# Expert weights of a decoder trunk loaded as 8 KB runs per partition, with strided transposes of the activations

## The chip, the core and the metric

The kernel runs on one core of a Trainium2 chip. Its time is the device time of one execution in microseconds (us). Before the change three runs took 1944.39, 1949.98 and 1954.2 us; the median is 1949.98 us.

The engines are named PE or TensorE (matrix products; PEld is its weight load), DVE or VectorE, ACT or ScalarE, POOL or GpSimd, and SP, which only issues transfers. Partition means one of the 128 rows of the on-chip memory.

## The reference

One inference step of a two-layer decoder trunk, for 512 prompt tokens and 32 sample tokens together (544 rows of 1024 channels). Each layer has a mixer, a cross attention over 256 memory tokens and a mixture of experts; after each comes a residual sum and a layer norm. The change touches the mixture of experts alone:

```python
def hier_moe(x, w_group, b_group, w_router, b_router, w_gate, w_up, w_down):
    ...                       # gates: a token's best group, its two best experts in it
    hg = jnp.einsum('md,edf->mef', xf, w_gate)     # 16 experts, d = 1024, f = 512
    hu = jnp.einsum('md,edf->mef', xf, w_up)
    hid = jax.nn.silu(hg) * hu * gates.astype(x.dtype)[..., None]
    y = jnp.einsum('mef,efd->md', hid, w_down)
```

All arrays are 32-bit floats. A product sums over all contraction rows, so the order in which these rows are dealt out to partitions is free, as long as both operands use the same order.

## The kernel before

Every matrix product is made from operands split in a high and a low part: for each weight tile ScalarE copies `raw` (128 x 2048) to `whi` in the product's rounded format (line 1308 in the expert loops), VectorE makes the rest, `wlo = raw - whi` (line 1685), and TensorE adds three products, hi x hi, lo x hi and hi x lo (line 924).

Weights come in units of 1 MB through a ring of four `raw` buffers. SP issues the loads in program order; a load into a buffer waits until VectorE has made the low part of the unit that was there before (`wait_release`). An expert has six units: two halves of `w_gate`, two of `w_up`, two of `w_down` (`expert_load`, line 461, issue at line 469). For `w_gate` a unit holds 512 contraction rows of 512 values, four rows on each partition; for `w_down` it holds 256 rows of 1024 values, two on each partition. In the kernel before, row `(u k p)` of an expert lies on partition p, so the rows of one partition are 128 rows apart in the memory outside: a gate or up unit is 512 runs of 2 KB, a down unit 256 runs of 4 KB.

Each expert handles up to 128 tokens. The order of one step of the loop over experts, on each engine: VectorE compares ranks to find the slots of a later expert (`hits`, line 1769) and turns TensorE's sums (line 901) into a list of token numbers (`tokens`, line 1778). GpSimd waits for this list, does a one-element operation (line 2176), and issues an indirect transfer that gathers 128 rows of 4 KB from the outside copy of the activations into `xg` (line 2177). TensorE transposes the gathered rows, 8 blocks of 128 x 128 (line 910); ScalarE and VectorE copy the blocks out as a high and a low part. TensorE then runs the gate and up products (48 matrix products of 512 columns), waits for the gathered rows of the next expert and transposes them, runs the down product of the expert before (24 products, line 924 too), transposes the hidden rows of this one (4 blocks, line 953), and sums the slots of the expert after next. VectorE forms the hidden rows (line 1799) after the split of the next expert's gate units. ScalarE writes the expert's result to `ye` (line 1356) and issues its store to `expert_rows` (line 1364). Steps are in program order on every engine, joined by counting semaphores; the loops are unrolled for the first three and last three experts and run in pairs between.

Tokens that don't fit in the 128 slots of an expert are handled after the loop, in `further` (lines 972 to 1035), with the same layout and unsplit products. In these data layer 1 has one such block.

A transpose is a product in which the data are the stationary operand and the identity matrix moves past it; the profile's names stand as moving, stationary.

Of the kernel before, what the change touches and what calls it, by code (L numbers as in the profile page):

```python
# [31 lines left out]
P = 128  # L32

def trunk_kernel(nc, a, outs):
    D = a["x_prompt"].shape[2]
# [5 lines left out]
    EXPERTS, FF = a["w_gate"].shape[1], a["w_gate"].shape[3]  # L42
# [6 lines left out]
    KC = D // P  # L49
# [150 lines left out]
    with ExitStack() as ctx:  # L200
# [25 lines left out]
        ident = sb("ident", [P, P])  # L226
# [37 lines left out]
        ps = ctx.enter_context(nc.psum_tensor("ps", [P, 8, 512], F32))  # L264
# [51 lines left out]
        xg = [area(1024 * i, 1024) for i in range(2)]  # L316
        silu = area(2048, 512)
        hid = area(2560, 512)
# [33 lines left out]
        A_, B_, C_, D_ = range(4)  # L352

        def pair_flat(i):
            return PAIR[i].rearrange("p b n -> p (b n)")

        def pair_chunks(i):
            return pair_flat(i).rearrange("p (k n) -> p k n", k=KC)
# [78 lines left out]
        @block.sync  # L437
        def _(sp):
            sp.dma_start(mem_rows, a["mem_prompt"][0].rearrange("(m p) n -> p m n", p=P)).then_inc(sig("mem_landed"), 16)
            i_raw = 0  # L440
            for u in UNITS:
                if u[0] == "unit":
                    _, key, src, wait_kv = u
                    if wait_kv:

                        for par in range(2):
                            sp.wait_ge(sig(f"kv_stored{par}"), 16 * 2 * DEPTH)
                    wait_release(sp, i_raw)
                    for dst, part in src(raw[i_raw % RING][:, :]):
                        sp.dma_start(dst, part).then_inc(sig(f"raw_landed{i_raw % RING}"), 16)  # L450
                    i_raw += 1
                    if key == ("wk0", 3):
                        sp.dma_start(h[:, 0:LASTT, :], a["x_prompt"][0].rearrange("(t p) n -> p t n", p=P)).then_inc(sig("x_landed"), 16)
                        sp.dma_start(h[0:NS, LASTT, :], a["x_sample"].rearrange("b t n -> (b t) n")).then_inc(sig("x_landed"), 16)
                    continue
                l, rb = u[1], i_raw
                w_gate = a["w_gate"][l].rearrange("e (u k p) n -> u e p k n", u=2, p=P)
                w_up = a["w_up"][l].rearrange("e (u k p) n -> u e p k n", u=2, p=P)
                w_down = a["w_down"][l].rearrange("e (u k p) n -> u e p k n", u=2, p=P)

                def expert_load(k, i, w, e):

                    wait_release(sp, rb + k, 12 * i)
                    slot = (rb + k) % RING
                    if isinstance(e, int):
                        src = w[e]
                    else:
                        src = w[bass.ds(e, 1)].rearrange("a p k n -> (a p) k n")
                    sp.dma_start(raw[slot][:, :].rearrange("p (k n) -> p k n", k=src.shape[1]), src).then_inc(sig(f"raw_landed{slot}"), 16)

                def load_step(c, i):
                    k, n = first_unit(c), c + 2 * i
                    if c < EXPERTS:
                        expert_load(k, i, w_gate[0], n)
                        expert_load(k + 1, i, w_gate[1], n)
                        expert_load(k + 2, i, w_up[0], n)
                        expert_load(k + 3, i, w_up[1], n)
                        k += 4
                    if c:
                        expert_load(k, i, w_down[0], n - 1)  # L480
                        expert_load(k + 1, i, w_down[1], n - 1)

                load_step(0, 0)
                for c in range(1, 3):
                    load_step(c, 0)
                with sp.Fori(0, EXPERTS // 2 - 3) as i:
                    load_step(3, i)
                    load_step(4, i)
                for c in range(EXPERTS - 3, EXPERTS + 1):
                    load_step(c, 0)  # L490
                i_raw += 6 * EXPERTS
                n = further_blocks(sp, l)
                def one_block(i):
                    e = sp.value_load(block_expert[0:1, i:i + 1] if isinstance(i, int) else block_expert[0:1, bass.ds(i, 1)], min_val=0, max_val=EXPERTS - 1)
                    for k, w in enumerate((w_gate, w_up, w_down)):
                        for q in range(2):
                            if k == 2:

                                sp.wait_ge(again(l, "used"), 2 + q + 6 * i)
                            elif isinstance(i, int):  # L500
                                wait_release(sp, i_raw + 2 * k + q)
                            elif k == q == 0:

                                sp.wait_ge(again(l, "used"), 1 + 6 * i)
                            src = w[q][bass.ds(e, 1)].rearrange("a p k n -> (a p) k n")
                            sp.dma_start(again_slot(l, 2 * k + q)[:, :].rearrange("p (k n) -> p k n", k=src.shape[1]), src).then_inc(again(l, f"landed{q}"), 16)

                with sp.If(n > 0):
                    one_block(0)
                with sp.If(n > 1):  # L510
                    with sp.Fori(1, FURTHER) as i:
                        with sp.If(n > i):
                            one_block(i)
                if l < DEPTH - 1:

                    sp.wait_ge(again(l, "used"), 1 + 6 * n)
# [3 lines left out]
        def _(pe):  # L520
# [110 lines left out]
            n = 0  # L631
# [259 lines left out]
            def experts(l):  # L891
# [12 lines left out]
                def gathered_columns(c, i):  # L904
                    n = c + 2 * i
                    pe.wait_ge(sig(f"gathered{c % 2}"), 16 * (l * EXPERTS // 2 + c // 2 + 1) + 16 * i)
                    if c:
                        pe.wait_ge(sig(f"xg{l}_lo"), past(f"xg{l}_lo") + n)
                    for k in range(KC):
                        mm = pe.transpose(pair_chunks(C_)[:, k, :], xg[c % 2][:, k * P:(k + 1) * P], ident[:, :])  # L910
                    mm.then_inc(sig(f"xg{l}_tr"), 1)

                def expert_product(k0, i, bank, hi, lo, k_unit, nbanks):
# [14 lines left out]
                def step(c, i):  # L928
                    n, k = c + 2 * i, first_unit(c)
                    if c < EXPERTS:  # L930

                        pe.wait_ge(sig(f"xg{l}_hi"), past(f"xg{l}_hi") + n + 1)
                        pe.wait_ge(sig(f"xg{l}_lo"), past(f"xg{l}_lo") + n + 1)
                        if c:
                            pe.wait_ge(sig(f"hid{l}"), past(f"hid{l}") + n)
                        expert_product(k, i, 0, xgT_hi, xgT_lo, 4, 1)
                        expert_product(k + 2, i, 1, xgT_hi, xgT_lo, 4, 1)
                        k += 4
                    if c < EXPERTS - 1:
                        gathered_columns(c + 1, i)  # L940
                    if c:

                        pe.wait_ge(sig(f"hid{l}_hi"), past(f"hid{l}_hi") + n)
                        pe.wait_ge(sig(f"hid{l}_lo"), past(f"hid{l}_lo") + n)
                        if c > 1:
                            pe.wait_ge(sig(f"ye{l}"), past(f"ye{l}") + n - 1)
                        expert_product(k, i, 2, hidT_hi, hidT_lo, 2, 2)
                    if c < EXPERTS:
                        pe.wait_ge(sig(f"hid{l}"), past(f"hid{l}") + n + 1)
                        if c:  # L950
                            pe.wait_ge(sig(f"hid{l}_lo"), past(f"hid{l}_lo") + n)
                        for k in range(4):
                            mm = pe.transpose(ps[:, 6, k * P:(k + 1) * P], hid[:, k * P:(k + 1) * P], ident[:, :])
                        mm.then_inc(sig(f"hid{l}_tr"), 1)
                    if c < EXPERTS - 2:
                        find_tokens(c + 2, i)
# [15 lines left out]
            def further(l):  # L972
# [3 lines left out]
                n = further_blocks(pe, l)  # L976
                def one_block(i):
# [9 lines left out]
                    pe.wait_ge(again(l, "copied"), 1 + 4 * i)  # L987
                    pe.wait_ge(again(l, "gathered"), 16 + 16 * i)
                    for k in range(KC):
                        mm = pe.transpose(pair_chunks(C_)[:, k, :], xg[0][:, k * P:(k + 1) * P], ident[:, :])  # L990
                    mm.then_inc(again(l, "tr"), 1)

                    pe.wait_ge(again(l, "copied"), 2 + 4 * i)
# [8 lines left out]
                            mm.then_inc(again(l, "used"), 1)  # L1002
                    pe.wait_ge(again(l, "hid"), 1 + i)
                    for k in range(4):
                        mm = pe.transpose(ps[:, 6, k * P:(k + 1) * P], hid[:, k * P:(k + 1) * P], ident[:, :])
                    mm.then_inc(again(l, "tr"), 1)

                    pe.wait_ge(again(l, "copied"), 3 + 4 * i)
# [1338 lines left out]
```

## Time and profile before

| | us |
|---|---|
| median of three runs | 1949.98 |
| lowest and highest | 1944.39, 1954.2 |
| span of the profiled execution (first to last instruction; the only time given of it) | 1949.7 |

| engine | busy us | share of the span | instructions |
|---|---|---|---|
| PE | 1591.0 | 82% | 8295 |
| PEld | 1278.4 | 66% | 8295 |
| DVE | 1178.7 | 60% | 1285 |
| ACT | 720.8 | 37% | 646 |
| POOL | 411.8 | 21% | 405 |

The two loops over experts lie at about 560 to 900 us and 1505 to 1850 us. The profile comes as a page and as a trace that can be asked for stretches, waits and the chain of work that ended last. The DMA share is the mean busy share of the core's 16 transfer engines; queue q1 carries what SP issues, q10 what ScalarE issues, q0 what GpSimd issues.

### The profile page before, as it was taken

Reading aid. Unit: us, or ns where it says so; the run is one execution under the profiler, and the core shown is the slowest. Engines: PE = TensorE matmul, PEld = TensorE weight load, DVE = VectorE, ACT = ScalarE, POOL = GpSimd, SP = SyncE. Lnnn points to the kernel's source line nnn. Section 1 sums busy time; section 2 is a strip of 40 time slices with the busy share of each in tenths; the row PEclk is TensorE's granted clock in tenths of the full one; section 3 lists DMA queues with packets and bytes.
Section 4 is the critical chain, followed back from the end, with each engine's and each line's share of the span. In section 5 each row is a group of like instructions: output and inputs, shape, how many; then the busy total and the mean of one; then the engine's idle time right before and its main releaser. Section 6 shows DMA issues by size and latency. Waiting matters only on the chain.

```text
span 1949.7 us, 21407 instructions
## 1 busy us (share of the span) xinstructions
PE 1591.0 (82%) x8295; PEld 1278.4 (66%) x8295; DVE 1178.7 (60%) x1285; ACT 720.8 (37%) x646; POOL 411.8 (21%) x405
## 2 busy tenths in 40 slices
PE   7989798899959999994496559898995899989860
PEld 5888478865647777773396557787673677777730
DVE  4333552341658788785779994513336787877636
ACT  4331321330236676673111112223202567666500
POOL 0101121000211001012689922300012000100006
PEclk9999798999979999997597779999998899999985
DMA  9730302066148999997411120203634699999822
GB/s 319 271 130 22 113 18 73 23 251 224 33 169 319 361 366 346 360 364 237 118 58 51 43 68 32 88 23 110 252 113 154 223 365 356 346 363 360 313 97 94
DMA packets 157539, 371.69 MB, mean 191 GB/s; under 512 B 8597, under 2 KB 38325, under 8 KB 157441
## 3 DMA queue, kind: packets, MB, share of 16 engines
q1 hardware_dynamic: 137200, 307.38, 44.9%
q0 software_dynamic: 12672, 44.76, 6.3%
q10 hardware_dynamic: 7585, 18.42, 2.6%
q8 instruction: 57, 0.93, 0.2%
q14 instruction: 25, 0.20, 0.0%
HBM read 342.54 MB, written 28.59 MB: 190 GB/s over the span
## 4 chain that ended last, share of the span: by engine, by line
PE 48%; DVE 21%; DMA 12%; issue 8%; POOL 4%; ACT 4%; ACTq 1%; DVEq 0%; SPq 0%; POOLq 0%
PE ps L543 15%; PE ps L924 10%; DMA arena<-h_rows,tok_of 6%; PE ps L560 6%; DMA raw<-in_w_gate_dram 4%; DVE arena L1969 3%; PE ps L832 3%; PE ps L847 3%; DVE arena L1967 3%; DVE wlo L1685 3%; DVE wlo L1481 2%; DVE xlo L1484 2%; ACT whi L1308 2%; PE ps L760 2%; PE ps L576 2%
## 5 line engine op out<-in xcount | busy, mean ns | idle before, releaser
L1685 DVE TENSOR_TENSOR wlo<-raw,whi 128x2048 fp32r<-128x2048 f32 x192 | 436.7, 2288 | 125.7 <-ACT whi L1308 124.9
L1308 ACT ACTIVATE whi<-raw 128x2048 fp32r<-128x2048 f32 x192 | 366.7, 1916 | 178.8 <-DMA raw<-in_w_gate_dram 86.9
L924 PE MATMUL ps<-whi,xhi 128*128 128x512 f32 x768 | 296.1, 413 | 18.2 <-issue 9.0
L924 PE MATMUL ps<-whi,xlo 128*128 128x512 f32 x768 | 287.4, 402 | 0.0
L924 PE MATMUL ps<-wlo,xhi 128*128 128x512 f32 x768 | 286.6, 400 | 0.0
L1481 DVE TENSOR_TENSOR wlo<-raw,whi 128x2048 fp32r<-128x2048 f32 x56 | 130.0, 2335 | 94.0 <-ACT whi L1151 94.0
L924 PEld LDWEIGHTS ps<-whi,xhi 128*128 128x128 f32 x768 | 147.1, 195 | 51.7 <-issue 18.0
L543 PE MATMUL ps<-whi,xhi 128*128 128x512 f32 (+1 forms) x528 | 170.1, 404 | 8.2 <-DVE wlo L1481 6.3
L924 PEld LDWEIGHTS ps<-whi,xlo 128*128 128x128 f32 x768 | 149.5, 195 | 34.1
L924 PEld LDWEIGHTS ps<-wlo,xhi 128*128 128x128 f32 x768 | 147.8, 192 | 35.6
L1484 DVE TENSOR_TENSOR xlo<-ps,xhi 128x1024 fp32r<-128x1024 f32 (+2 forms) x112 | 110.0, 983 | 97.3 <-ACT xhi L1155 34.4
L543 PE MATMUL ps<-wlo,xhi 128*128 128x512 f32 (+1 forms) x528 | 165.8, 395 | 0.0
L543 PE MATMUL ps<-whi,xlo 128*128 128x512 f32 (+1 forms) x528 | 165.4, 394 | 0.0
L560 PE MATMUL ps<-xhi,whi 128*128 128x272 f32 x544 | 119.0, 302 | 47.9 <-DVE rt L1987 46.6
L2176 POOL TENSOR_TENSOR wait_mark<-minus_half 1x1 f32<-1x1 f32 x32 | 29.1, 911 | 555.0 <-DVE tok_of L1778 541.6
L1151 ACT ACTIVATE whi<-raw 128x2048 fp32r<-128x2048 f32 x56 | 106.3, 1911 | 87.4 <-PE ps L560 61.3
L560 PEld LDWEIGHTS ps<-xhi,whi 128*128 128x128 f32 x544 | 90.5, 200 | 49.3 <-DVE rt L1987 47.9
L560 PE MATMUL ps<-xlo,whi 128*128 128x272 f32 x544 | 117.5, 299 | 0.0
L1155 ACT ACTIVATE xhi<-ps 128x1024 fp32r<-128x1024 f32 (+1 forms) x32 | 28.9, 905 | 238.5 <-PE ps L528 238.5
L560 PE MATMUL ps<-xhi,wlo 128*128 128x272 f32 x544 | 116.9, 297 | 0.0
L543 PEld LDWEIGHTS ps<-whi,xhi 128*128 128x128 f32 (+1 forms) x528 | 93.0, 180 | 36.2 <-issue 9.0
L543 PEld LDWEIGHTS ps<-whi,xlo 128*128 128x128 f32 (+1 forms) x528 | 94.0, 178 | 30.0
(319 smaller groups left out, 2347.2 us busy)
## 6 DMA issues: line engine op xcount, KB each, us to landing
raw<-in_w_gate_dram SPq DMA_DIRECT2D x66, 1024.0 KB, 7.4
raw<-in_w_up_dram SPq DMA_DIRECT2D x66, 1024.0 KB, 7.8
raw<-in_w_down_dram SPq DMA_DIRECT2D x66, 1024.0 KB, 7.4
raw<-in_cache_mem_k_dram SPq DMA_DIRECT2D x16, 1024.0 KB, 5.3
raw<-in_cache_mem_v_dram SPq DMA_DIRECT2D x16, 1024.0 KB, 5.6
expert_rows<-arena ACTq DMA_DIRECT2D x32, 512.0 KB
raw<-in_w_k_dram SPq DMA_DIRECT2D x8, 1024.0 KB, 8.6
raw<-in_w_v_dram SPq DMA_DIRECT2D x8, 1024.0 KB, 10.3
```

What stands on the lines that cost most here:

```text
L543: mm = pe.matmul(ps[0:m, 2 * pair + half, :], x[:, k, lhs_cols], w[s % RING][:, at:at + 512], start=(k == 0 and n == 0), stop=(k == KC - 1 ...
L560: mm = pe.matmul(ps[:, 2 * pair + half, 0:MOVE], w[s % RING][:, at:at + P], x[:, k, half * MOVE:(half + 1) * MOVE], start=(k == 0 and n == ...
L832: mm = pe.matmul(pair[0:NS, hh * NMEM:(hh + 1) * NMEM], q_only[:, j, b, :], KT[(b + 1) % 2][:, j, :], start=(b == 0 and j in (0, 4)), stop ...
L847: mm = pe.matmul(pair_flat(A_)[0:NS, hh * HD:(hh + 1) * HD], p_only[:, 2 * hh + m, b, :], vb[:, m, hh * HD:(hh + 1) * HD], start=(b == 0 a ...
L924: mm = pe.matmul(ps[:, bank + half, :], x[:, k, :], w[s][:, at:at + 512], start=(k == 0 and n == 0), stop=(k == 2 * k_unit - 1 and n == 2))
L1151: act.activation(whi[s % RING][:, :], raw[i % RING][:, :], ACT.Copy).then_inc(sig("hi_made"), 1)
L1308: act.activation(whi[s % RING][:, :], raw[r % RING][:, :], ACT.Copy).then_inc(sig("hi_made"), 1)
L1481: dve.tensor_tensor(wlo[s % RING][:, :], raw[i % RING][:, :], whi[s % RING][:, :].bitcast(F32), ALU.subtract).then_inc(sig("lo_made"), 1)
L1484: return dve.tensor_tensor(out, full, hi.bitcast(F32), ALU.subtract)
L1685: dve.tensor_tensor(wlo[s % RING][:, :], raw[r % RING][:, :], whi[s % RING][:, :].bitcast(F32), ALU.subtract).then_inc(sig("lo_made"), 1)
L1967: written["p"] = link.mark(dve.scalar_tensor_tensor(p_out, p_in, w, p_out, ALU.mult, ALU.add))
L1969: ins = dve.scalar_tensor_tensor(s_out, s_in, w, s_out, ALU.mult, ALU.add)
```

## The change

The rows of an expert are dealt to the partitions in another order: partition p takes 8 rows of `w_gate` and `w_up` (4 of `w_down`) that follow each other, and a unit takes half of them. Each partition's share of a unit is then one run of 8 KB. To match, block k of the transposed activations holds channels k, k + 8, k + 16 and so on (for the hidden rows k, k + 4, ...) in place of 128 that follow each other.

```diff
-                w_gate = a["w_gate"][l].rearrange("e (u k p) n -> u e p k n", u=2, p=P)
-                w_up = a["w_up"][l].rearrange("e (u k p) n -> u e p k n", u=2, p=P)
-                w_down = a["w_down"][l].rearrange("e (u k p) n -> u e p k n", u=2, p=P)
+                w_gate = a["w_gate"][l].rearrange("e (p u k) n -> u e p k n", u=2, p=P)
+                w_up = a["w_up"][l].rearrange("e (p u k) n -> u e p k n", u=2, p=P)
+                w_down = a["w_down"][l].rearrange("e (p u k) n -> u e p k n", u=2, p=P)
...
-                        mm = pe.transpose(pair_chunks(C_)[:, k, :], xg[c % 2][:, k * P:(k + 1) * P], ident[:, :])
+                        mm = pe.transpose(pair_chunks(C_)[:, k, :], xg[c % 2][:, k:D:KC], ident[:, :])
...
-                            mm = pe.transpose(ps[:, 6, k * P:(k + 1) * P], hid[:, k * P:(k + 1) * P], ident[:, :])
+                            mm = pe.transpose(ps[:, 6, k * P:(k + 1) * P], hid[:, k:FF:4], ident[:, :])
```

The two transposes of the extra blocks (lines 990 and 1005) change in the same way.

## Rows read from the trace of the kernel before

**Rows 1.** The page's chain that ended last, share of the span by line.
```profile
PE ps L543 15%; PE ps L924 10%; DMA arena<-h_rows,tok_of 6%; PE ps L560 6%; DMA raw<-in_w_gate_dram 4%; DVE arena L1969 3%; PE ps L832 3%; PE ps L847 3%; DVE arena L1967 3%; DVE wlo L1685 3%; DVE wlo L1481 2%; DVE xlo L1484 2%; ACT whi L1308 2%; PE ps L760 2%; PE ps L576 2%
```
**Rows 2.** Busy us (instructions) per engine, clock, DMA share, GB/s: the expert loops.
```profile
620.00:900.00 280.00, 259.60 (x1210) 208.83 (x1208) 221.80 (x146) 190.37 (x135) 28.23 (x25) 0.98 1.00 356
...
1560.00:1810.00 250.00, 230.90 (x1077) 186.17 (x1076) 201.61 (x134) 172.43 (x122) 27.05 (x24) 0.97 0.98 355
```
**Rows 3.** Chain in order of time, two experts of layer 0: start us, us, what.
```profile
778.05 8.96 DMA raw<-in_w_gate_dram
...
791.27 0.68 DVE arena L1799
...
796.19 2.32 POOL wait_mark L2176
...
798.65 9.10 DMA arena<-h_rows,tok_of
...
807.79 1.09 PE ps L910 x8
808.88 5.58 PE ps L924 x24
...
816.22 1.92 ACT whi L1308
...
820.48 6.95 DMA raw<-in_w_gate_dram
```
**Rows 4.** The chain in both expert loops: first and last transfers on it.
```profile
594.86 6.39 DMA arena<-h_rows,tok_of
...
615.49 7.34 DMA raw<-in_w_gate_dram
...
1504.56 4.26 DMA arena<-h_rows,tok_of
...
1540.13 6.44 DMA arena<-h_rows,tok_of
...
1725.67 7.25 DMA raw<-in_w_gate_dram
...
1784.80 8.88 DMA arena<-h_rows,tok_of
```
**Rows 5.** Waits in 620:900 of PE and ACT: us in total, times, longest.
```profile
PE ps L910 <- DMA arena<-h_rows,tok_of: 12.2, 6, 2.9
...
ACT whi L1308 <- DMA raw<-in_w_gate_dram: 37.8, 21, 3.4
```
**Rows 6.** DMA in 1181:1192, where a cache copy of 8 blocks runs.
```profile
DMA packets 320, 1.47 MB, mean 134 GB/s; under 512 B 56, under 2 KB 56, under 8 KB 312
```
**Rows 7.** DMA in 235:238 (1 KB), 643:646 (2 KB) and 10:16 (4 KB).
```profile
DMA packets 1096, 1.11 MB, mean 369 GB/s; under 512 B 15, under 2 KB 1096, under 8 KB 1096
...
DMA packets 598, 1.20 MB, mean 399 GB/s; under 512 B 18, under 2 KB 18, under 8 KB 598
...
DMA packets 660, 2.50 MB, mean 416 GB/s; under 512 B 50, under 2 KB 50, under 8 KB 660
```
**Rows 8.** DMA queues (packets, MB, share) in 804:805, then in 50.5:51.5.
```profile
q0 software_dynamic: 66, 0.27, 69.0%
q1 hardware_dynamic: 63, 0.13, 34.2%
...
q0 software_dynamic: 54, 0.22, 53.7%
q1 hardware_dynamic: 51, 0.21, 50.7%
```
**Rows 9.** Instructions of lines 910, 1713 (16-byte steps), 1756: ns min/median/max, starts, forms.
```profile
L910 PEld LDWEIGHTS ps<-ident,arena x256: 137/141/231, 563.8 to 1815.5; 128*128 128x128 f32 x128
...
L1713 DVE TENSOR_REDUCE picked<-arena x2: 289/290/290, 551.8 to 1497.3; 128x20 f32<-128x80 f32 x2
...
L1756 DVE TENSOR_REDUCE rt<-arena x4: 235/236/236, 561.3 to 1508.1; 128x5 f32<-128x80 f32 x4
```

More of the change, by code:

```diff
@@ L989, in one_block @@
                     for k in range(KC):
-                        mm = pe.transpose(pair_chunks(C_)[:, k, :], xg[0][:, k * P:(k + 1) * P], ident[:, :])
+                        mm = pe.transpose(pair_chunks(C_)[:, k, :], xg[0][:, k:D:KC], ident[:, :])
                     mm.then_inc(again(l, "tr"), 1)
@@ L1004, in one_block @@
                     for k in range(4):
-                        mm = pe.transpose(ps[:, 6, k * P:(k + 1) * P], hid[:, k * P:(k + 1) * P], ident[:, :])
+                        mm = pe.transpose(ps[:, 6, k * P:(k + 1) * P], hid[:, k:FF:4], ident[:, :])
                     mm.then_inc(again(l, "tr"), 1)
```

## The prediction

> **What bounds the kernel now.** I read the chain of waits first, then the stretches, then the waits of single engines, and last the DMA queues. The page's chain says that no engine holds the end alone; among its largest pieces stand the gather of token rows (6% of the span) and the load of expert gate weights (4%), both transfers of the expert loops [rows 1]. The change lives in those two loops. There the DMA engines are busy all the time (share 1.00 and 0.98, 356 and 355 GB/s) and TensorE is busy 259.60 of 280 us and 230.90 of 250 us, so both have little left [rows 2]. An expert lasts 20.4 us: the gather of the third expert of layer 1 starts at 1540.13, that of the fifteenth at 1784.80 [rows 4].
>
> A piece of the chain, two experts long, shows the loop that sets the pace [rows 3]. Weights land (8.96 us), are split by ScalarE and VectorE, VectorE makes the hidden rows, then the token list; GpSimd marks (2.32) and issues the gather; the gather lands after 9.10 us; TensorE transposes the gathered rows (1.09), does the down product (5.58); the split of the next weights frees a slot, and the next gate load goes out. So the path passes through two transfers per pair of experts, a weight load and a gather. The same alternation runs through both loops: 12 gathers that meet weights stand on the chain from 594.86 to 1784.80, together 101.8 us, 8.5 each, and 10 weight loads from 615.49 to 1725.67, together 77.2 us, 7.7 each [rows 4]. The gather at 1504.56, which meets no weight stream, needs 4.26 us, half of the others. In the loop of layer 0 TensorE waits for the gather in every second expert, 12.2 us in six waits, and ScalarE for gate weights, 37.8 us in 21 [rows 5].
>
> **The change, part by part.**
>
> *Fewer, longer packets.* A gate or up load is 512 runs of 2 KB now and 128 of 8 KB after; a down load 256 of 4 KB and then 128 of 8 KB. A run of that length can be one packet: in the stretch with the cache copy (8 blocks of 53 KB) all but 312 of 320 packets are under 8 KB, so the eight blocks are one packet each [rows 6]. What a packet costs beyond its bytes I take from three full streams: 369 GB/s with 1 KB packets, 399 with 2 KB, 416 with 4 KB [rows 7]. Over 16 engines that is 44.4, 82.1 and 157.5 ns a packet, which is a straight line: 37.7 ns per KB and 6.7 ns fixed. An 8 KB packet is then an estimated 308 ns (426 GB/s). A 1 MB load takes 32 packets an engine x 82.1 = 2.63 us now and 8 x 308 = 2.46 after, 0.16 less; a down load 2.52 to 2.46. Per expert 4 x 0.16 + 2 x 0.06 = 0.76 us, 24 us over 32 experts: that is the whole gain if the transfers alone set the pace. On the chain only the 10 weight legs count. Each waits for about two loads' worth of moving (2 x 0.16 = 0.3), and loses less to gathers that cut in (next paragraph; up to 0.65 us). I take 0.6 a leg: -6 us (bounds 0 and -10).
>
> *The gather against longer packets.* Two queues that both have work share an engine packet by packet, not byte by byte. Where 4 KB rows meet 4 KB rows, 54 and 51 packets pass in one us and each side gets half the time; where gathered 4 KB rows meet 2 KB weights, 66 and 63 packets pass, and the gather gets 69.0% against 34.2% [rows 8]. So the gather is favoured today because its packets are the longer ones. After the change they are the shorter ones. An engine carries 8 rows of a gather. Now that is 8 x (0.167 + 0.087) = 2.0 us (times per packet from the same rows: 69.0% of 16 us over 66, 34.2% over 63); after, 8 x (0.167 + 0.308) = 3.8 us. So a gather that meets weights lands 1.8 us later. In the experts where it is already late, nothing hides this: TensorE stands at the transposes behind it, in order, and the down product, the hidden rows' transposes and the token search of the next experts are queued behind those. 12 legs x 1.8 = +21.6 us. Bounds: 0 if a long run gives way inside itself as often as now, and 12 x 3 = +36 if rows in flight ahead of the first one add as much again. The write of expert rows is slowed in the same way, but nothing waits for it in the loop.
>
> A part comes back: with each pair of experts longer by some 1.6 us of 41, the streams have 4% less to carry per us, and the two legs (7.7 and 8.5 us) shorten by about that: 0.65 a pair, -8 us over 12 pairs. This is an estimate; the bounds are 0 and -16.
>
> *Strided transposes.* The gathered rows and the hidden rows are the stationary operand, so the stride falls on the weight load of TensorE: 141 ns for 128 columns today, all contiguous [rows 9]. No row shows a strided load on TensorE. The nearest is VectorE reading the same memory: a reduction over 80 values 16 bytes apart takes 290 ns, over 80 adjacent ones 236 [rows 9], 0.67 ns a value more, though it also writes 20 results and not 5. For 128 columns that is 86 ns a load. Bounds: 0, and a doubling of the load (141 ns). I take 86, because it is the only row that differs by the stride. There are 12 such loads per expert, but only the 8 behind a gather that is on the chain count in full: 14 legs (the 12 and the first of each loop) x 8 x 0.086 = +9.6 us, and 12 in the extra block of layer 1, +1.0. The other loads lie in experts where TensorE has the 2 to 3 us of its next wait for a gather as cover; without it they would cost another 14 us. The Trainium skill, page "SBUF — State Buffer", section Specifications (TRN2), says that memory lines are 16 bytes and that full bandwidth needs at least two hits in a line; both new strides (32 and 16 bytes) put each value in a line of its own, so by the page the loads slow down, by an amount that it doesn't give, and without that rule the sum is 10 us lower. No run here shows it for TensorE.
>
> *Unchanged.* Buffers, semaphores, the order of issue on SP and POOL and the number of DMA instructions stay. The splits of weights read the same contiguous 128x2048 tiles.
>
> Sum: -6 + 21.6 - 8 + 9.6 + 1.0 = +18 us on the profiled span of 1949.7, which lies 0.3 us under the median of the runs shown (1949.98): 1968 us.
>
> **The rivals.**
> 1. *Faster: the stream sets the pace.* The share of 1.00 speaks for it, and ScalarE's waits for gate weights. Then the 0.76 us per expert come through, and the gather loses little because the weights are further ahead: -24 us without stride cost, 1926. The limit is TensorE, busy 92.5% of the loop. Against it: single weights are waited for by ScalarE, hardly by TensorE [rows 5]. It decides if a gather under load still lands in 9 us or less. Chance 0.28.
> 2. *No change.* The packets save on the weight leg what the gather loses: gather +0.7 us (as beside 4 KB packets: 8 x (0.167 + 0.157) = 2.6 against 2.0), so 12 x 0.6 = +7, -6 for the weight legs, no stride cost: 1951. The same number comes out if the runs stay cut at 2 KB, so that the change doesn't do what it says, and the loads of TensorE don't care for the stride. Chance 0.18.
> 3. *Slower by TensorE.* The strided load takes twice its time, 141 ns x 12 = 1.7 us an expert. TensorE has 1.5 us idle per expert (280 - 259.60 us over 280 / 20.4 experts), so it becomes the bound in both experts of a pair, with the gather's delay on top: 1968 + 32 x 1.7 - 10 = about 2012. For it: every value in another line. Against it: the load overlaps the multiplication before it. Chance 0.12.
>
> The forecast itself has 0.42.
>
> **How the numbers follow.** What a measurement of this kernel can tell from no change is about 0.5%, 10 us. The forecast's own range, from the bounds of its four terms (half widths 5, 18, 8 and 6, squared, summed and rooted: 21), is 1947 to 1989, so about 0.04 of its 0.42 lies within 0.5% of before. Slower by more than that: 0.38 and rival 3, 0.50; within: 0.18 and 0.04, 0.22; faster: 0.28. For 8 in 10 the range must reach into rival 1 and most of the way to rival 3: 1926 to 2006.
>
> **What would show it.** Packets of 8 KB in the expert loops, some 28,700 fewer per layer (16 experts x (4 x 384 + 2 x 128)). One us in which gather and weights meet should show equal packet counts but the gather at about a third of the time; gathers under load at 10 to 11 us; weight loads at 7 us or a little less; the wait of TensorE for the gather at twice its 12.2 us. The loads of lines 910 and 953 at 200 to 230 ns and not 140. The forecast is wrong if gathers land as before or the waits of TensorE shrink, and its stride part if those loads still take 140 ns.

## The result and the profile after

The changed kernel takes 1956.64 us (median of 20 runs, 1947.9 to 1963.6), the kernel before 1950.76 (20 runs). The ratio is 1.0039, 95% interval 1.0021 to 1.0057: slower by 4 to 11 us. The forecast was slower by 18 us, 1968. The profiled execution has a span of 1957.9 us against 1949.7.

The chain of the page names the place. The columns are those of [rows 1]:

```profile
PE ps L543 16%; PE ps L924 8%; DMA arena<-h_rows,tok_of 8%; PE ps L560 6%; DMA raw<-in_w_gate_dram 4%; DVE arena L1969 3%; DVE wlo L1685 3%; PE ps L832 3%; PE ps L847 3%; DVE arena L1967 3%; ACT whi L1308 3%; DVE wlo L1481 2%; DVE xlo L1484 2%; PE ps L760 2%; PE ps L910 2%
```

The gather went from 6% to 8% of the chain, and line 910, the transposes that wait for it, came into the list. The windows of the two loops, columns as in [rows 2]:

```profile
620.00:900.00 280.00, 258.81 (x1186) 210.62 (x1185) 219.84 (x145) 190.01 (x133) 26.28 (x25) 0.96 0.94 352
...
1566.00:1816.00 250.00, 227.66 (x1051) 185.85 (x1050) 195.58 (x130) 169.20 (x118) 25.54 (x24) 0.95 0.93 347
```

Fewer instructions of TensorE fit in the same window (1186 for 1210 in layer 0), the transfer engines have become idle 6% of the time, and the bytes per us have fallen a little, 356 to 352. So the packets did get cheaper (the price of a megabyte stands below), and yet no more bytes pass. How long each loop lasts shows from the transposes of the hidden rows, one group of four per expert. Line 953, columns: ns min/median/max, first and last start, forms; before, layer 0 and layer 1:

```profile
L953 PE MATMUL ps<-ident,arena x64: 270/273/330, 582.9 to 892.3; 128*128 128x128 f32 x64
...
L953 PE MATMUL ps<-ident,arena x64: 270/272/330, 1528.2 to 1839.8; 128*128 128x128 f32 x64
```

and after:

```profile
L953 PE MATMUL ps<-ident,arena x64: 272/284/386, 580.3 to 893.4; 128*128 128x128 f32 x64
...
L953 PE MATMUL ps<-ident,arena x64: 272/284/387, 1529.4 to 1847.7; 128*128 128x128 f32 x64
```

First to last start is 309.4 and 311.6 us before, 313.1 and 318.3 after: 10.4 us more in the two loops; the rest of the program lies 2.2 us the other way.

The packets are what the diff says (page, section on queues; before there were 157539 packets):

```profile
DMA packets 98403, 371.69 MB, mean 190 GB/s; under 512 B 8597, under 2 KB 38325, under 8 KB 72961
```

The chain of waits in both loops, start us, us, what; first the gather that meets no weights, then the first and last of those that do, and the first and last weight leg (they answer to [rows 4]):

```profile
1505.77 4.27 DMA arena<-h_rows,tok_of
...
592.31 6.68 DMA arena<-h_rows,tok_of
...
1792.26 9.80 DMA arena<-h_rows,tok_of
...
613.31 6.53 DMA raw<-in_w_gate_dram
...
1773.49 7.43 DMA raw<-in_w_gate_dram
```

There are 14 gathers that meet weights on the chain, 139.9 us together, 10.0 each (before 12, 8.5 each), and 12 weight legs, 81.9 us, 6.8 each (before 10, 7.7 each). So not only the length of a leg changed, but their number: gather and weight load now alternate without a gap through both loops, where the chain of before skips a gather in places (gate loads at 675.86 and 694.80 follow each other). The free gather is as it was, 4.27. TensorE's and ScalarE's waits in 620:900, us in total, times, longest, beside [rows 5]:

```profile
PE ps L910 <- DMA arena<-h_rows,tok_of: 17.2, 6, 3.8
...
ACT whi L1308 <- PE ps L924: 32.0, 31, 3.7
ACT whi L1308 <- DMA raw<-in_w_gate_dram: 30.1, 19, 2.9
```

The wait for the gather is up by 5.0 us, ScalarE's wait for gate weights down by 7.7: waiting moved from the one transfer to the other. The strided loads show in line 910's records, 193 ns for the 141 of [rows 9]:

```profile
L910 PEld LDWEIGHTS ps<-ident,arena x256: 185/193/231, 560.9 to 1823.8; 128*128 128x128 f32 x128
```

### The profile page after: what moved, and what is told of

It is laid out like the page before. It is cut to its first block, busy times and chain, and to the rows that moved or that the text cites. A ratio compares the mean times of both kernels' runs of the same rounds, so it can differ in the third digit from the quotient of the medians.

```text
span 1957.9 us, 21407 instructions
## 1 busy us (share of the span) xinstructions
PE 1596.4 (82%) x8295; PEld 1286.2 (66%) x8295; DVE 1178.4 (60%) x1285; ACT 722.1 (37%) x646; POOL 408.3 (21%) x405
## 4 chain that ended last, share of the span: by engine, by line
PE 47%; DVE 22%; DMA 14%; issue 7%; ACT 5%; POOL 4%; ACTq 0%; DVEq 0%; POOLq 0%; SPq 0%
PE ps L543 16%; PE ps L924 8%; DMA arena<-h_rows,tok_of 8%; PE ps L560 6%; DMA raw<-in_w_gate_dram 4%; DVE arena L1969 3%; DVE wlo L1685 3%; PE ps L832 3%; PE ps L847 3%; DVE arena L1967 3%; ACT whi L1308 3%; DVE wlo L1481 2%; DVE xlo L1484 2%; PE ps L760 2%; PE ps L910 2%
## 5 line engine op out<-in xcount | busy, mean ns | idle before, releaser
L2176 POOL TENSOR_TENSOR wait_mark<-minus_half 1x1 f32<-1x1 f32 x32 | 17.9, 558 | 567.5 <-DVE tok_of L1778 554.1
## 6 DMA issues: line engine op xcount, KB each, us to landing
raw<-in_w_v_dram SPq DMA_DIRECT2D x8, 1024.0 KB, 10.6
```

## The experiments

The theory: a gather that meets 8 KB runs lands 1.5 us later, on the chain 0.9 us per weight leg comes back, and the strided loads of TensorE cost nothing because they hide. Rival A: the stride makes the time. Rivals B to G stand with the runs for which they were written. All ratios are against the kernel before on the same chip; they and their intervals come from all runs of both kernels and need not be the ratio of the two medians.

**The changed kernel again**, as the base of this set.

> The changed kernel as it is, as the base for the others on the same chip. All theories: 1.003 to 1.005 of the kernel before (about +6 us). Gathers that meet weights at 10.0 us on the chain (8.5 before), weight legs at 6.8 us (7.7 before).

1961.36 us, ratio 1.0041 (1.0010 to 1.0072). Twelve gathers that meet weights are on the chain, 9.8 us each, and seven weight legs of 7.2 us. The amount of the loss holds; the legs of single executions differ by some tenths.

**Stride alone.**

```diff
-                w_gate = a["w_gate"][l].rearrange("e (p u k) n -> u e p k n", u=2, p=P)
+                w_gate = a["w_gate"][l].rearrange("e (p k u) n -> u e p k n", u=2, p=P)
...
-    xg[c % 2][:, k:D:KC]
+    xg[c % 2][:, 2 * (k % 4) + k // 4:D:KC]
```

(`w_up`, `w_down` and the other three transposes in the same way.)

> Stride without length: the rows of a partition are dealt so that the transposes are strided as in the change, but the runs stay 2 KB (gate, up) and 4 KB (down), as before. Theory (the gather loses the favoured half of the transfer engines to longer runs, and the strided loads hide behind the transpose before them): as the kernel before, 1951 +- 3 us, gathers under load back at 8.5 us, equal packet counts of gather and weights where they meet, the wait of TensorE for the gather in layer 0's loop near 12 us; loads of lines 910 and 953 at 185 to 210 ns all the same. Rival A (the stride on TensorE makes the time): as the changed kernel, 1957 us, with gathers at 8.5 us. Rival B (the +6 us are a shift of which experts fall late, not tied to either part): anything between 1945 and 1960 with gathers at 8.5 to 9.

1948.89 us, 0.9995 (0.9968 to 1.0021). Every transpose is strided, its load is recorded as long as in the changed kernel, and nothing is lost:

```profile
L910 PEld LDWEIGHTS ps<-ident,arena x256: 185/193/231, 565.5 to 1811.4; 128*128 128x128 f32 x128
```

Ten gathers under load are on the chain, 7.8 us each, 0.7 us under the kernel before at an equal time; so a mean of some ten legs can move by that much without the length of the gate runs. Rival A falls, and so does the forecast's +10.6 us for the stride: the interval allows -6 to +4.

**Half the length.**

```diff
-                w_gate = a["w_gate"][l].rearrange("e (p u k) n -> u e p k n", u=2, p=P)
+                w_gate = a["w_gate"][l].rearrange("e (p g u j) n -> u e p g (j n)", u=2, g=2, p=P)
```

(`w_up` alike, `w_down` as in the run above, the transposes to match.)

> Half the length: strided as in the change, all weight runs 4 KB. Theory in its present form (a long run gives way about every 4 KB): the gather shares as beside 8 KB runs, so gathers at 9.5 to 10 us, one packet of weights for one of the gather, time 1955 to 1958 us. Rival C (a run of 8 KB passes whole, as the prediction had it): gathers here near 9 us (8 x (0.167 + 0.157) = 2.6 us an engine against 2.0 before), clearly below the 10.0 of 8 KB runs, and 1952 to 1954 us. Rival A: 1957 us with gathers at 9.

1970.07 us, 1.0095 (1.0057 to 1.0133): slower than with 8 KB, which none of the theories had. Gathers on the chain take 8.9 us, as rival C said, so their length doesn't explain it. More of this below.

**Length without stride, in layer 1.**

```diff
-    xg[c % 2][:, k:D:KC]
+    xg[c % 2][:, k * P:(k + 1) * P] if l else xg[c % 2][:, k:D:KC]
```

> Length without stride, in layer 1 alone: runs of 8 KB everywhere, but layer 1's transposes read contiguous columns (so layer 1's expert products pair other channels with the weight rows than the reference does; the amount of work and the routing are the same). Theory: as the changed kernel within 2 us (eight transposes behind a gather 1.09 and not 1.16 us, 0.07 x 7 legs), gathers of layer 1 still near 10.5 us. Rival A: layer 1's loop, 7 us longer in the change from its third to its last expert (272.8 against 265.8 us), gets these 7 us back, so the time is back at 1950 to 1951 us.

(The hidden rows and the extra block in the same way.) 1960.69 us, 1.0061 (1.0035 to 1.0088): by the medians 0.7 us under the changed kernel of the same set, by the ratios 0.2% above it, so nothing is regained. The recorded loads of line 910 go from 137 ns (layer 1) to 193 (layer 0) in one kernel, and TensorE waits for layer 1's gathers as long as in the changed kernel (18.8 us there):

```profile
PE ps L910 <- DMA arena<-h_rows,tok_of: 19.8, 7, 3.8
```

What the stride costs where it is on the chain can be read directly. Eight transposes and the products behind them, changed kernel, layer 0 (strided, start us, us, what):

```profile
765.06 1.16 PE ps L910 x8
766.22 5.57 PE ps L924 x24
```

and this kernel, layer 1 (contiguous):

```profile
1635.88 1.09 PE ps L910 x8
```

The recorded load grows by 52 ns, eight transposes in a row by 0.07 us, 9 ns each. That holds at TensorE's full clock. Behind many waits for a gather it runs at half of it (last section), and where it does so throughout, eight take 1.97 us strided or not; in the kernel before (contiguous) for example:

```profile
642.95 1.97 PE ps L910 x8
```

**Only `w_down` in 8 KB runs** (gate and up as before).

> Only w_down in 8 KB runs (hidden rows transposed with stride), gate and up as before in 2 KB runs; a third of the weight bytes change. Theory (long runs stretch the time in which a gather's rows pass): gathers on the chain at 8.5 to 9 us, those that meet a down load longest; time between before and the changed kernel, 1950 to 1954 us. Rival D (the loss has another cause than the gather, and goes with the bytes in long runs): a third of +8 us, 1952 us, with gathers at 8.5 us. Both give nearly one time, the legs tell them apart.

1956.02 us, 1.0031 (1.0007 to 1.0056). Gathers on the chain 8.7 us (13 legs), weight legs 7.8: the gate loads that are on the chain give nothing back here, and the gather loses 0.2 us a leg. That makes less than the 8 us between the medians, but the interval reaches down to 1.4 us, and the execution with these legs, 1969.01 us, was the slowest of the twelve. The run doesn't tell the theories apart.

**The gather taken off the chain.** On TensorE the token search of expert c + 2 moves from the end of the step to right behind the gate and up products, on VectorE the token list from the start of the next step to right behind the hidden rows. GpSimd then issues the gather earlier: by the packet records of the kernels with 2 KB runs, in layer 0's loop, its first row starts 7.5 to 11.1 us ahead of the transposes that use it and not 2.4 to 5.0 (some 5 us more, and not the 10 that were expected). Two kernels: this edit on the changed kernel and on the kernel before.

```diff
                         k += 4
+                    if c < EXPERTS - 2:
+                        find_tokens(c + 2, i)
                     if c < EXPERTS - 1:
                         gathered_columns(c + 1, i)
...
-                    if c < EXPERTS - 2:
-                        find_tokens(c + 2, i)
...
-                    if c and c < EXPERTS - 1:
-                        tokens(c + 1, i)
...
                     dve.tensor_tensor(hid, silu, ps[:, 1, :], ALU.mult).then_inc(sig(f"hid{l}"), 1)
+                    if c < EXPERTS - 2:
+                        tokens(c + 2, i)
```

> The changed kernel, with the token search and the token list of expert c + 2 moved forward by about half an expert (right behind the gate and up products and behind the hidden rows), so that the gather is issued some 10 us earlier against its use. Theory: the gather leaves the chain, TensorE's wait for it in layer 0's loop falls from 17 us to under 4 us, gathers may take 10 us or more without harm, and the saved packet time comes through: DMA share back to 0.97 or more, time 1920 to 1940 us, and faster than the same edit on the kernel before by 8 to 24 us. Rival D: the long runs cost something besides the gather, so this kernel is not faster than the same edit on the kernel before. Rival E (TensorE or the splits hold the loop anyway): waits for the gather vanish, but the time stays within 5 us of the changed kernel.

> The same move of the token search in the kernel before (2 KB and 4 KB runs, contiguous transposes). Theory: there the transfer engines have a share of 1.00 already, so taking the gather off the chain gives little: 1940 to 1950 us, with the wait for the gather gone and ScalarE's wait for gate weights up from 37.8 us. Rival E: as much gain as with long runs or none in both.

With 8 KB runs 1913.31 us, 0.9819 (0.9780 to 0.9857); with the runs of before 1914.36, 0.9820 (0.9786 to 0.9854). The wait for the gather is gone from TensorE's list in 620:900, with 8 KB runs:

```profile
PE ps L924 <- DVE xlo L1484: 4.7, 5, 1.8
PE ps L924 <- issue: 4.5, 8, 0.7
PE ps L955 <- DVE arena L1797: 1.0, 3, 0.4
```

No gather that meets weights is left on the chain of either. They land even later now, and it does no harm: medians of 12 in 620:900, DMA issues, columns out<-in, engine, operation, count, us to landing; 8 KB first, then 2 KB:

```profile
arena<-h_rows,tok_of POOLq DMA_INDIRECT x12, 10.0
```

```profile
arena<-h_rows,tok_of POOLq DMA_INDIRECT x12, 8.5
```

Three things follow. The loss of the changed kernel goes when its gather is covered. The cheaper packets don't turn into time even then: the gate legs on the chain take 8.1 us (14 legs) with 8 KB and 8.0 (15 legs) with 2 KB, and the two kernels have one time, where the theory had 8 to 24 us between them. That is the sign that was written for rival D; whether the saved packet time is worth nothing there or another cost of the long runs eats it up, these runs don't tell. Rival E's reason, that TensorE or the splits hold the loop anyway, falls: both kernels run some 35 us under the kernel before. And my expectation for the kernel before was wrong by 25.6 us or more: I took the share of 1.00 for a full stream. With the same 2 KB runs, the same share and the gather covered, more bytes pass (366 and 370 GB/s against the 356 and 355 of [rows 2]):

```profile
620.00:900.00 280.00, 250.26 (x1180) 199.23 (x1178) 225.28 (x150) 197.08 (x138) 20.73 (x29) 0.97 1.01 366
...
1566.00:1816.00 250.00, 233.72 (x1112) 186.27 (x1110) 204.67 (x142) 173.86 (x123) 19.63 (x29) 0.99 1.00 370
```

The covered loops end earlier, at about 875 and 1798, so these windows hold some of what follows. A window inside both loops shows it more clearly, before and then covered, both with 2 KB runs:

```profile
620.00:840.00 220.00, 204.20 (x965) 164.88 (x964) 179.85 (x121) 154.08 (x109) 26.18 (x22) 0.98 0.99 358
```

```profile
620.00:840.00 220.00, 209.43 (x1000) 167.09 (x999) 189.06 (x127) 163.52 (x116) 13.62 (x24) 0.99 1.02 379
```

**Addresses against length.** 4 KB runs had lost more than 8 KB runs. In all the layouts above with 4 or 8 KB gate runs, a unit is made of alternate pieces of 2 MB. These three make each unit one contiguous megabyte (two of them), or keep the spaced 4 KB runs and cover the gather.

```diff
-    "e (p u k) n -> u e p k n"            # 8 KB runs, 16 KB apart
+    "e (u p k) n -> u e p k n"            # 8 KB runs, contiguous unit
...
-    "e (p g u j) n -> u e p g (j n)"      # 4 KB runs, 8 KB apart
+    "e (u g p j) n -> u e p g (j n)"      # 4 KB runs, contiguous unit; w_down as before
```

> 8 KB runs as in the change, but a unit is one contiguous megabyte (partition p of unit u takes rows 512 u + 4 p to 512 u + 4 p + 3) in place of 128 runs 16 KB apart; transposes read every 4th (hidden: every 2nd) column. Theory (the length of a run is what delays the gather): as the changed kernel, 1.003 to 1.006 of before, gathers on the chain at 10 us. Rival F (the addresses, alternate pieces of 2 MB, slow the loads and not the length): back to the time before, gathers at 8.5 us.

> 4 KB runs for gate and up with each unit one contiguous megabyte; down as before. Earlier, 4 KB runs 8 KB apart gave 1.0095, more than 8 KB runs did, with gathers at only 8.9 us and weight legs at 8.0. Theory (length alone): the same 1.007 to 1.012. Rival F (addresses): 1.000 to 1.004, weight packets passing at 170 us or less per thousand and not 181, weight legs at 7.5 us.

> The 4 KB runs 8 KB apart with the early token search. Theory (whatever the length, the loss passes through the gather on the chain): as the two other kernels with the early search, 1914 +- 4 us, 0.980 to 0.984. Rival F (the 4 KB loads themselves are slow): the loss of 18 us stays, 1925 to 1935 us.

8 KB, contiguous: 1957.94 us, 1.0032 (1.0010 to 1.0055), gathers 10.0 us (14 legs), weight legs 7.1. Here no effect of the addresses shows, and that of the length does. Every kernel with 8 KB gate runs and the gather on the chain loses (1.0032 to 1.0061), stride alone doesn't; against rival B, the loss goes with the length.

4 KB, contiguous: 1944.49 us, 0.9976 (0.9954 to 0.9999), gathers 9.0 us (11 legs), gate legs 7.1 (8 legs); faster than the theory and rival F both had it. With the length kept and the spacing gone (that of `w_down` too), 1.2% of the time comes back, some 23 us. Spaced first, then contiguous, window 620:900 (queue q1: packets, MB, share; issues as above):

```profile
q1 hardware_dynamic: 24478, 84.50, 83.8%
...
raw<-in_w_gate_dram SPq DMA_DIRECT2D x24, 1024.0 KB, 8.4
...
arena<-h_rows,tok_of POOLq DMA_INDIRECT x12, 8.7
```

```profile
q1 hardware_dynamic: 29786, 86.95, 84.2%
...
raw<-in_w_gate_dram SPq DMA_DIRECT2D x24, 1024.0 KB, 7.7
...
arena<-h_rows,tok_of POOLq DMA_INDIRECT x12, 7.6
```

A megabyte takes 83.8% x 280 us x 16 / 84.50 = 44.4 us of engine time spaced and 43.4 contiguous (44.1 and 42.6 in 620:840, which lies inside both loops), and gate loads and gathers land 0.7 and 1.1 us later when spaced. But 44.4 is no more than the 45.1 of the kernel before with 2 KB runs, so the price of a megabyte alone doesn't make the spaced kernel slower than that one.

4 KB, spaced, gather covered: 1946.53 us, 0.9987 (0.9968 to 1.0005), against 1914 for the other layouts. So this layout is slow even without the gather on the chain, as rival F had it and the theory not, and by more than rival F had it (1925 to 1935). ScalarE waits longer for down weights than in the four other kernels with the gather covered (41.4 us against 12.8 to 30.6), and TensorE for the hidden rows (13.5 against 1.0 to 3.0):

```profile
ACT whi L1308 <- DMA raw<-in_w_down_dram: 41.4, 17, 3.6
ACT whi L1308 <- DMA raw<-in_w_gate_dram: 19.9, 23, 2.0
...
PE ps L955 <- DVE arena L1797: 13.5, 13, 1.8
```

Why pieces of 4 KB at a distance of 8 KB are slow and pieces of 8 KB at 16 KB are not stays open. The distance alone isn't it: in the run with stride alone `w_down` already lay in 4 KB pieces 8 KB apart, its loads landed as before (7.5 us), and nothing was lost.

**Contiguous units with the gather covered**, 8 KB and then 4 KB runs.

> 8 KB runs of contiguous units with the early token search. Theory: with the gather off the chain neither length nor stride counts, 1914 +- 4 us. Rival F: some us faster than the early search with 8 KB runs 16 KB apart, 1905 to 1910 us.

> 4 KB runs of contiguous units, the fastest layout without the early token search (0.9976), with it. Theory (with the gather off the chain the length of a run doesn't count, only badly spaced 4 KB runs do): as with 2 KB and 8 KB runs, 0.980 to 0.984, 1910 to 1917 us. Rival G (the gain of contiguous 4 KB runs comes from the loads and not from the gather, so it adds to the early search): 0.977 to 0.980, 1904 to 1910 us. Weight packets of the loads at a mean of 174 us per thousand, as without the early search.

1913.91 us, 0.9818 (0.9789 to 0.9848), and 1915.26 us, 0.9825 (0.9793 to 0.9857). Both medians lie with the theory and outside the ranges of rivals F and G, though both intervals reach into these. Four kernels with the gather covered, with runs of 2, 4 and 8 KB, lie within 2 us, where the same layouts with the gather on the chain spread from 0.9976 to 1.0041. Each interval is some 0.35% wide to either side, so a remainder of a few us can't be excluded for any one of them.

## Why the prediction was wrong in size

The direction and the place hold, and the other terms hold as a net change per leg; the step that failed is "Strided transposes", a term of +10.6 us that measured 1 us or less.

*Fewer, longer packets, and the gather against them: right by the leg, the sum in part by luck.* The forecast had a gather at +1.8 us less half of the 0.65 us per pair that comes back, so about +1.5 a leg, and a weight leg at -0.6 with the other half, about -0.9. Measured: 8.5 to 10.0 and 7.7 to 6.8. These terms alone, -6 + 21.6 - 8, make +7.6 us, or 1957.3; the runs give 1956.64. But they were summed over 12 gathers and 10 weight loads, and the chain of after has 14 and 12: the legs of both kinds grew from 179.0 to 221.8 us together, 42.8 more, while the span grew by 8.2, because other work left the chain in their place. The sum has no term for that; that it comes out to a microsecond is in part luck. The price of the bytes was right too: weights took 86.08 MB in 86.6% of the window before, 45.1 us of engine time a MB, and take 84.87 MB in 80.9%, 42.7, after: 5% less, as the straight line through [rows 7] says for four gate and up units (2.63 to 2.46) and two down units (2.52 to 2.46). The shortest 8 KB packets of the weight loads in the window take 307 ns, where 308 was estimated; their mean is 342.

*Strided transposes: +9.6 and +1.0 forecast, 1 or less measured.* The step took VectorE's 0.67 ns per value for a term of the end time, one load after the other. The loads did grow, by 52 ns in line 910 and 69 in line 953 (86 forecast), but strided loads of 193 ns follow each other every 145 ns (eight in 1.16 us), so the records overlap, and eight in a row took 1.16 us for 1.09. Over 14 legs that is 1 us at most, since at half the clock it is nothing. Two runs show it from both sides: stride without length 0.9995, length without stride in layer 1 no faster than the change. The trace of before could have told: eight transposes take 1.09 us [rows 3], 136 ns each, less than one recorded load of 141 [rows 9], so the records already overlapped, and a longer record need not be a longer pitch. The Trainium skill, "Perfetto Trace Analysis", section "Per-instruction lifecycle: what the profiler-reported window actually captures", says that the end of a TensorE instruction in a profile is worked out from its size and a memory delay, and isn't observed. These traces fit that (193 ns recorded, 145 from one to the next): the pitch is the number to sum, not the record. Two slips of that step leave the forecast where it is: its loads without cover come to 23 us by its own figures (272 of 0.086 us) and not 14, and the half width of its term to 8 and not 6.

*The gather is right by its legs, its mechanism isn't shown.* I expected equal packet counts where rows meet long runs, the gather at a third of the time. One us of the changed kernel (802:803; packets, MB, share) shows two rows to one run and the gather ahead:

```profile
q0 software_dynamic: 48, 0.20, 57.6%
q1 hardware_dynamic: 24, 0.16, 37.8%
```

Slices at 1630 and 1716 look the same (40 to 23, 51 to 25). By the forecast's own sum these counts make 8 x (0.192 + 0.126) = 2.5 us an engine against 2.0, a third of the 1.5 us by which the legs grew; so that one for one gave nearly the right size is luck as far as such slices show. Over the whole passage it looks otherwise. By the packet records of the legs on the chain, from first to last row 2.8 weight runs pass for each row before and 1.1 after, and the rows have 43% and 33% of the engines' time. That passage lasts 3.3 us before, 3.7 (contiguous 4 KB) and 4.5 (8 KB); the rest of the leg, ahead of the first row and behind the last, 5.2 to 5.5 in all of them. So the delay grows with the length of a run and lies among the rows. How an engine shares within it is not settled. The wait of TensorE for the gather, forecast at twice its 12.2 us, came to 17.2.

*Rival 1, the stream sets the pace:* no. Gathers under load land in 10.0 us and not in 9 or less; cheaper packets made the engines idle (share 1.00 to 0.94), and with the gather covered they still bought nothing that shows. The Trainium skill, "Perfetto Trace Analysis", section "DMA Optimizations", advises to go from 2 KB to 4 or 8 KB a transfer where the memory is busy and transfers set the bound. The bytes did get cheaper here, by 5%, but the time rose by 0.39%; the chain holds the delay of single transfers. *Rival 2* (1951) lies outside the interval of the difference, though its stride cost of nothing was right. *Rival 3* asked for TensorE in both experts of a pair; its idle time in the window even grew, from 20.4 to 21.2 us.

## What to carry to other kernels

Making one stream's packets longer can take service from a smaller transfer that meets it; look whether such a transfer is on the chain, and issue it earlier first: here that was worth some 35 us, and afterwards the run length no longer told, but for the spaced 4 KB layout. Price a change to a pipelined instruction by the pitch of a row of them, not by the length of one record. A DMA share of 1.00 did not mean here that no more bytes would pass: 358 GB/s at 0.99 became 379 at 1.02 with the same runs.

## What the runs showed of the hardware

- A TensorE weight load of 128 32-bit values in steps of 32 bytes is recorded at 193 ns, in steps of 16 bytes at 209, contiguous at 141 and 140 (medians of lines 910 and 953); with contiguous 4 KB units, where line 910 reads in steps of 8 bytes, also at 209. The closest step was not the cheapest.
- All expert weights in runs of 4 KB placed 8 KB apart cost 1.2% of this kernel's time against contiguous ones (1.0095 to 0.9976), and 1.6% with the gather covered (0.9987 to 0.9825).
- After a wait for a gather TensorE can run at half its clock (1.2 of 2.4 GHz). In the changed kernel a wait of 3.56 us ended at 1634.88; the columns are those of the windows above, the clock third from the end:

```profile
1635.00:1637.00 2.00, 2.00 (x9) 1.98 (x10) 0.33 (x1) 1.75 (x2) 0.00 (x0) 0.50 1.01 426
1641.00:1645.00 4.00, 4.00 (x25) 3.38 (x24) 1.60 (x1) 2.62 (x2) 0.00 (x0) 1.00 0.58 227
```

The eight transposes there took 1.97 us and not 1.16. The kernel before has such stretches too (1.97 at 642.95). That is part of what a late gather costs: the mean clock of the loops went from 0.98 and 0.97 to 0.96 and 0.95. It was no term of the forecast.
